# Sharing out the low parts of the expert weights: GpSimd every third half slot, VectorE the others

## The reference

```python
def moe_swiglu(h, router_w, w_gu, w_down):
    probs = jax.nn.softmax((h @ router_w).astype(jnp.float32), axis=-1)
    top_p, top_i = lax.top_k(probs, TOP_K)
    top_p = top_p / jnp.sum(top_p, axis=-1, keepdims=True)
    ...
    for e in range(N_EXPERTS):
        y = y + gates[..., e:e + 1] * swiglu(h, w_gu[e], w_down[e])
```

## Time and profile before

| | |
|---|---|
| median of 3 runs | 2228.12 us (2222.12 to 2228.62) |
| span of the profiled execution | 2218.5 us |
| mean granted TensorE clock | 0.969 of full speed |
| the experts, first to last matmul | 1422.5 to 2159.8 us |
| busy PE / PEld | 2013.3 / 1505.1 us (91% / 68%) |
| busy DVE / ACT / POOL | 957.6 / 734.1 / 775.3 us |
| bytes moved | 320.03 MB |

### The profile page before, as it was taken

The page is one execution under the profiler, slowest core; times in us unless marked ns, Lnnn a source line. Parts: engine busy times, 40 slices in busy tenths (PEclk is TensorE's granted clock), DMA queues, the critical chain, the costliest instruction groups (busy, mean ns, idle before and its releaser), DMA issues. The chain is left out here.

```text
span 2218.5 us, 38581 instructions
## 1 busy us (share of the span) xinstructions
PE 2013.3 (91%) x14384; PEld 1505.1 (68%) x14385; DVE 957.6 (43%) x1610; ACT 734.1 (33%) x1216; POOL 775.3 (35%) x475
## 2 busy tenths in 40 slices
PE   5999999999998699999999998889999899899990
PEld 2446776777676546888788876667786686678770
DVE  2204665666566445432412228553333434332228
ACT  1112332243233102222122211454445545544331
POOL 0016324422442202112112223564446546543234
PEclk7999999999999899999999999999999999999995
DMA  7212234223321434324322350886658758765354
GB/s 259 76 53 88 82 95 128 82 73 108 120 74 61 162 114 132 105 86 136 114 96 86 100 178 5 282 295 183 209 181 268 242 180 276 245 191 167 110 176 151
DMA packets 257672, 320.03 MB, mean 144 GB/s; under 512 B 25401, under 2 KB 197697, under 8 KB 257435
## 3 DMA queue, kind: packets, MB, share of 16 engines
q1 hardware_dynamic: 242571, 285.01, 40.2%
q10 hardware_dynamic: 10832, 16.96, 2.2%
q0 software_dynamic: 4032, 14.68, 1.7%
HBM read 283.93 MB, written 32.65 MB: 143 GB/s over the span
## 5 line engine op out<-in xcount | busy, mean ns | idle before, releaser
L1335 POOL TENSOR_TENSOR wlo<-wring,whi 128x1024 fp32r<-128x1024 f32 x182 | 462.6, 2544 | 748.8 <-ACT whi L1771 685.1
L1121 PE MATMUL pp<-whi,xTh 128*128 128x512 f32 (+1 forms) x1152 | 446.4, 387 | 29.2 <-POOL wlo L1335 10.2
L1771 ACT ACTIVATE whi<-wring 128x1024 fp32r<-128x1024 f32 (+1 forms) x324 | 315.1, 980 | 438.5 <-PE pp L1123 361.3
L1123 PE MATMUL pp<-wlo,xTh 128*128 128x512 f32 (+1 forms) x1152 | 431.3, 374 | 0.0
L1122 PE MATMUL pp<-whi,xTl 128*128 128x512 f32 (+1 forms) x1152 | 430.4, 374 | 0.0
L2356 DVE TENSOR_TENSOR wlo<-wring,whi 128x1024 fp32r<-128x1024 f32 (+1 forms) x180 | 223.9, 1244 | 207.5 <-ACT whi L1771 120.8
L1121 PEld LDWEIGHTS pp<-whi,xTh 128*128 128x128 f32 x1152 | 218.1, 189 | 85.6 <-POOL wlo L1335 21.7
L1123 PEld LDWEIGHTS pp<-wlo,xTh 128*128 128x128 f32 x1152 | 217.9, 189 | 39.4
L1122 PEld LDWEIGHTS pp<-whi,xTl 128*128 128x128 f32 x1152 | 218.7, 190 | 34.0
L1121 PE MATMUL pp<-whi,hTh 128*128 128x512 f32 x528 | 212.2, 402 | 7.7 <-POOL wlo L1335 2.9
L739 PE MATMUL pp<-xT,wring 128*128 128x512 f32 x384 | 205.0, 616 | 2.0 <-ACT scratch L1572 2.0
(11 more groups left out here) (316 smaller groups left out, 2667.0 us busy)
## 6 DMA issues: line engine op xcount, KB each, us to landing
wring<-in_moe_w_gu SPq DMA_DIRECT2D x320, 256.0 KB, 3.9
wring<-in_ada_w SPq DMA_DIRECT2D x80, 512.0 KB, 4.5
wring<-in_moe_w_down SPq DMA_DIRECT2D x160, 256.0 KB, 3.4
wring<-in_ffn_w_gu SPq DMA_DIRECT2D x80, 256.0 KB, 3.1
wring<-in_dn_w_in SPq DMA_DIRECT2D x96, 128.0 KB, 3.3
wring<-in_ffn_w_down SPq DMA_DIRECT2D x40, 256.0 KB, 3.0
expert_in<-zeros SPq DMA_DIRECT2D x36, 256.0 KB, 3.2
wring<-in_ada_w SPq DMA_DIRECT2D x32, 256.0 KB, 5.9
```

The lines of the kernel that those rows point to most:

```text
L1121: pe.matmul(out, hi[:, c0 + c, tt], wh, start=(first and c == 0), stop=False)
L1123: mm = pe.matmul(out, hi[:, c0 + c, tt], wl, start=False, stop=(last and c == nk - 1))
L1335: pool.tensor_tensor(wlo[:, hs, 0:nk, 0:w], wring[:, ring_p.slot(k), 2:2 + nk, 0:w], whi[:, hs, 0:nk, 0:w].bitcast(F32), ALU.subtract).the ...
L1771: act.activation(whi[:, hs, 0:nk, 0:w], wring[:, ring_v.slot(k), 2 * s:2 * s + nk, 0:w], ACT.Copy)\
```

## The change

Each half of an expert's weights has one maker by its number: GpSimd if m % 3 == 2, VectorE otherwise, over all eight experts (36 halves each, and 36 is a multiple of 3). Two semaphores, `low_by_dve` and `low_by_pool`, replace the pair of the layer, and `low_count` says which count half m of expert e has; PE, SP's fills and its end wait by them. The first lows are 0, 1 and 3 on VectorE and 2 on GpSimd. On VectorE the third low of a group comes ahead of `products`. In the down part a VectorE low of half 28 + m stands at step m itself. The `If`s of `silus` are nested: the first tile that the expert doesn't have ends the test. Layer 0's dense part keeps the even/odd split.

```diff
+def pool_half(m):
+    return m % 3 == 2
+
+def low_count(m, e=0):
+    if pool_half(m):
+        return m // 3 + 1 + e * 12
+    return m + 1 - (m + 1) // 3 + e * 24
...
@@ sync, fill @@
-                    if l is not None:
-                        sp.wait_ge(slot_split[l][half], k + 1 + i * per)
+                    if l == 0:
+                        sp.wait_ge(slot_split[half], k + 1 + i * per)
+                    elif l and (i or k >= RING):
+                        sp.wait_ge(low_sem(2 * k + half), low_count(2 * k + half - 2 * RING, i))
...
@@ tensor, half @@
-                    pe.wait_ge(slot_split[l][s], split_count(k, e))
+                    if l:
+                        pe.wait_ge(low_sem(m), low_count(m, e))
+                    else:
+                        pe.wait_ge(slot_split[s], split_count(k, e))
...
@@ gpsimd @@
-            low_halves(1, 0, 2)
+            low(1, 2, 0, low_by_pool)
...
-            low_halves(1, 2, 146)
+            for i in range(5, 292, 3):
+                low(1, i % 36, i // 36, low_by_pool)
...
@@ scalar, silus @@
-                        if t == 0 or l == 0:
+                        if l == 0:
                             one()
-                        else:
-                            with act.If(n > t):
-                                one()
+                    if l:
+                        def deeper(t):
+                            b = t if j % 2 == 0 or t > 1 else 5 + t
+                            act.wait_ge(f["gu_ps"], q0 + (t + 1))
+                            act.activation(hbuf[:, t, 0:w], bank(b)[:, 0:w], ACT.Silu).then_inc(f["sil_done"], 1)
+                            if t + 1 < T:
+                                with act.If(n > t + 1):
+                                    deeper(t + 1)
+                        deeper(0)
...
@@ vector, expert @@
+                def own_lows(lo, hi, e):
+                    for m in range(lo, hi):
+                        if not pool_half(m):
+                            low(m // 2, e, m % 2)
...
-                        low(2 * j + 2, e)
+                        if l:
+                            own_lows(4 * j + 4, 4 * j + 7, e)
+                        else:
+                            low(2 * j + 2, e)
                         products(c * 6 + n * j, n, j)
-                        low(2 * j + 3, e)
+                        if l:
+                            own_lows(4 * j + 7, 4 * j + 8, e)
+                        else:
+                            low(2 * j + 3, e)
...
-                        if m % 2 and (l or e == 0 or m < 8):
+                        if l:
+                            own_lows(28 + m, 29 + m, e)
+                        elif m % 2 and (e == 0 or m < 8):
                             low(14 + m // 2, e)
...
@@ vector, ahead of the router @@
-            for k in range(2):
-                dve.wait_ge(S["slot_hi"], hi_count(1, 2 * k))
+            for m in (0, 1, 3):
+                k, s = m // 2, m % 2
+                dve.wait_ge(S["slot_hi"], hi_count(1, m))
```

More of the change, by code:

```diff
@@ L332, in backbone, with low_sem @@
                                           "xTh_ready", "xTl_ready") if l or n not in ("xs_in", "y_out")} for l in range(2)]
-        slot_split = [[sem(f"slot_split_{half}{l}") for half in ("first", "second")] for l in range(2)]
+        slot_split = [sem(f"slot_split_{half}") for half in ("first", "second")]
+        low_by_dve, low_by_pool = sem("low_by_dve"), sem("low_by_pool")
+        def low_sem(m):
+            return low_by_pool if pool_half(m) else low_by_dve
         yg_in = [sem(f"yg_in{t}") for t in range(T)]
@@ L585, in _ @@
                 for half, pieces in enumerate(parts(ring.slot(k))):
-                    for split in slot_split[0]:
+                    for split in slot_split:
                         sp.wait_ge(split, 37 + k)
@@ L620, in _ @@
             for k in range(2):
-                for split in slot_split[1]:
-                    sp.wait_ge(split, k + 1 + 18 * 8)
-                for half in slot_loaded[ring.slot(k)]:
+                for s, half in enumerate(slot_loaded[ring.slot(k)]):
+                    sp.wait_ge(low_sem(2 * k + s), low_count(2 * k + s - 2 * RING, 8))
                     sp.sem_inc(half, 32)
@@ L1324, in _, with low @@
             pool.wait_ge(S["pool_const"], 1)
[L1326 to L1341, removed]
+            def low(l, m, e, done):
+                k, s = m // 2, m % 2
+                nk = half_rows(k, s)
+                w = 256 if k in (10, 11) else 512
+                hs = m % HALVES
+                pool.wait_ge(S["slot_hi"], hi_count(l, m, e))
+                pool.tensor_tensor(wlo[:, hs, 0:nk, 0:w], wring[:, ring_of[l].slot(k), 2 * s:2 * s + nk, 0:w],
+                                   whi[:, hs, 0:nk, 0:w].bitcast(F32), ALU.subtract).then_inc(done, 1)
+            pool.sem_inc(slot_split[1], RING)
             pool.wait_ge(S["pool_const"], 2)
@@ L1458, in _ @@
                 pool.tensor_tensor(rstd[:, 1, t:t + 1], rstd[:, 0, t:t + 1], mhalf[:, 0:1], ALU.pow).then_inc(S["ln_rstd"], 1)
-            low_halves(0, 0, 36)
+            for i in range(36):
+                low(0, 2 * (i % 18) + 1, i // 18, slot_split[1])
             pool.wait_ge(S["gs_in"], 32)
@@ L1964, in _ @@
                     dve.sem_inc(F[l][n], 1)
-                dve.sem_inc(slot_split[l][0], RING)
+            dve.sem_inc(slot_split[0], RING)
             def add_mod(b, out):
@@ L2350, in ffn, with low @@
                 ring_v = ring_of[l]
-                def low(k, e):
+                def low(k, e, s=0):
+                    nk = half_rows(k, s)
                     w = 256 if k in (10, 11) else 512
[L2354 to L2357, removed]
+                    hs = (2 * k + s) % HALVES
+                    dve.wait_ge(S["slot_hi"], hi_count(l, 2 * k + s, e))
+                    dve.tensor_tensor(wlo[:, hs, 0:nk, 0:w], wring[:, ring_v.slot(k), 2 * s:2 * s + nk, 0:w],
+                                      whi[:, hs, 0:nk, 0:w].bitcast(F32), ALU.subtract)\
+                        .then_inc(low_by_dve if l else slot_split[0], 1)
+                def own_lows(lo, hi, e):
+                    for m in range(lo, hi):
+                        if not pool_half(m):
+                            low(m // 2, e, m % 2)
                 def xs_low(i, t, g, b):
@@ L2537, in _ @@
             w8 = slice(4, 12)
-            for k in range(2):
-                dve.wait_ge(S["slot_hi"], hi_count(1, 2 * k))
-                dve.tensor_tensor(wlo[:, 2 * k, :, :], wring[:, ring_of[1].slot(k), 0:2, :],
-                                  whi[:, 2 * k, :, :].bitcast(F32), ALU.subtract).then_inc(slot_split[1][0], 1)
+            for m in (0, 1, 3):
+                k, s = m // 2, m % 2
+                dve.wait_ge(S["slot_hi"], hi_count(1, m))
+                dve.tensor_tensor(wlo[:, m, :, :], wring[:, ring_of[1].slot(k), 2 * s:2 * s + 2, :],
+                                  whi[:, m, :, :].bitcast(F32), ALU.subtract).then_inc(low_by_dve, 1)
             dve.wait_ge(S["once_ps"], 7 + T)
```

## The result

Over 20 runs of each, the changed kernel takes 2229.0 us (2225.83 to 2235.95) and the kernel before 2225.1: **ratio 1.0021, 95% interval 1.0014 to 1.0029**. So it is 0.2% slower, some 4 us: within the 0.3% that the prediction called no change, though clear of 1. Predicted were 11.2 us less. The profiled execution spans 2226.8 us and took 2228.6, 1.8 more. The 9.6 us that the prediction had added to the span of before was thus no constant: the execution profiled there was a short one (with the same 1.8 it took an estimated 2220.3 us). Single profiles must be read with that in mind: of the 8.3 us between the two spans only about 4 are the change.

The account below looks back on a forecast made before the run. In one-tile experts, GpSimd's and VectorE's lows taking turns, with transfers close behind. Capped by transfers, gate/up saves 5.4, 2.9 and 2.1 us, down 0.5 and 0.3, sum 11.2, other terms 0: 2228.1 to 2216.9 us, range 2203 to 2228.

Parts of the forecast that it names:

- What bounds the kernel: One-tile experts 0, 3 and 5: PE's weight loads wait 26.1 us for GpSimd's lows, which take turns with VectorE's; transfers close behind.
- So the floor of the turns falls from at most 39.8 to about 35.2: One-tile gate/up: four full turns go from 2.24 to 1.08, 4.6 us less; 13.9 over three if nothing else were close.
- At most 2.22 if GpSimd has its turn, still hidden: Experts of two or three tiles: a VectorE low blocked by GpSimd takes at most 2.22 us, hidden behind PE's 2.7 per half.
- Transfers, the cap: One-tile stretches shrink only until the DMA share is 0.95: gate/up 5.4, 2.9, 2.1 us less, down 0.5, 0.3; sum 11.2.
- VectorE's order: Gate/up's third low ahead of products, refill asked for earlier; in experts of two or three tiles nothing gained or lost.
- rival B: One-tile down parts: nine VectorE lows at 1.23 ahead of xTl eat the gain, 11.1, or refills stay late; 2228.0; chance 0.20.
- Nested silus: ACT's tests in the experts: one instead of four with one tile; at most 7.4 us of ACT time, counted as 0.
- SP's queue: Refill transfers keep number and order, cost 0; a late VectorE low delays later refills by at most 2.22 us per ring turn.
- Ahead of the router: VectorE makes three lows instead of two, 5.5 us, 1.0 more, hidden in its 2.15 us of idle time.
- Experts of more tiles: Experts of two or three tiles: lows hidden behind PE, nothing gained or lost; two-tile stretches stay at 65 us.
- rival C: The lows ahead of xTl also bite in experts with more tiles: 27.1 over 22 steps, less 11.2; 2244.0 us; chance 0.08.
- Rival A: No cap: transfers go over 0.95, PE becomes the bound in gate/up; 22.0 us less, 2206.1; chance 0.22.

Follow-up runs that it names:

- half the bytes: Each expert weight transfer loads half its bytes, the rest of the slot keeps what lay there; ratio to before 0.9948 on the kernel before, 0.9972 on the changed kernel.
- the down order: In the down part VectorE makes hTl and xTl ahead of the step's low: changed kernel 1.0009, all lows on VectorE 0.9964, ratios to before.
- the two pairs of the table: Without and with the down order: changed kernel 1.0021 and 1.0009; all lows on VectorE 0.9994 and 0.9964.

## Why the prediction was wrong

The sign of the forecast was wrong, and 2229.0 lies 1.0 us past the upper end of its range. Its outcome "within 0.3%" had 0.22. By its own steps:

**What bounds the kernel** held: the largest moves were in experts 0, 3 and 5, and GpSimd's lows were on the path there. Taking away their reading was worth 10.2 us.

**"So the floor of the turns falls from at most 39.8 to about 35.2": this step failed.** It priced the exchange as throughput, 1.66 against 1.47 us a half. But the turns don't run back to back; in a one-tile gate/up part they stand in a ring with the transfer, ACT's high part and PE's matmuls, each waiting for the last. The gate/up parts fell by 2.5 us where the sum had 10.4 of its 11.2. What counts there is who is blocked when, and the blocking hardly shrank, from 56.1 to 52.2 us; PE's waits for lows stayed at 20 us (the prediction's outer bound, 34.7, was read from the weight loads' waits; PE's own were 20.1). The price of the turns on the whole was 10.2 us before and 11.6 after, where the sum had 11.2 to 13.9 less. Worse, a GpSimd that is blocked holds up only its own low; a blocked VectorE holds up hTl, the products and xTl behind it. "At most 2.22 if GpSimd has its turn, still hidden" was granted for experts of two and three tiles and priced nowhere for those of one tile, and in expert 3 alone VectorE stood blocked for 11.6 us instead of 4.3.

**"Transfers, the cap" was never reached**, and with it went the size of the sum. The gate/up share stayed at 0.88, and with half the bytes the split cost the same 0.24%. As a figure for full, 0.95 was fair: the gate/up parts of the version with all lows on VectorE and the down order, where no turns are left, have 0.93 and 0.96 in experts 0 and 3. In that version the next limit may well be as close as the prediction said; under the changed kernel's turns and order nothing pressed against it.

**"VectorE's order" at 0 failed too:** the down parts of one tile grew by 8.0 us. The forecast left it to rival B, which had the right place and mechanism. Rival B priced nine lows at 1.23, 11.1 us; the runs show 6.7 us where VectorE makes all lows and some 2.7 (not resolved by itself) in the changed kernel. It also missed that step 0 puts a low ahead of the last hTl, and so PE's wait for hTl at L1104 went from 0.3 to 5.0 us. Here is that place in expert 3, VectorE, then PE:

```profile
1727.63 3.23 DVE L2382 TENSOR_TENSOR wlo<-wring,whi 128x1024 fp32r<-128x1024 f32 x2 [0.94 <-ACT whi L1790]
1730.78 0.28 DVE L2402 TENSOR_TENSOR hTl<-pp,hTh 128x128 f32 x1
```

```profile
1731.11 0.66 PE L1104 MATMUL pp<-cm,x 128*128 128x128 f32 x4 [0.76 <-DVE hTl L2402]
```

Two lows stand ahead of hTl, 3.23 us together where two free ones take 2.44, and PE idles for 0.76 us. In the kernel before only one low, half 26's, stands between the last products and hTl.

**Nested silus at 0** held (0.9997). **SP's queue at 0** is contradicted by no run, but the chain after has 7.5% for SP (L461) where before had 2.7%: that points to refills held behind a late low of VectorE, but it wasn't tried by itself. **Ahead of the router** held: the three lows took 5.65 us, 5.5 expected. **Experts of more tiles** held within 2 us (544.3 to 546.2), and rival C did not come. But its steps are not free there: the down order takes 1.6 and 3.7 us off these experts in the two pairs of the table. **Rival A** failed even with the transfers' cap out of play: at half the bytes, the split still gained nothing.

**Of the signs listed**, the number of GpSimd's lows (96) and the 65 us stretches came as said. The mean of these lows over both widths, which the earlier trace rows gives as 2.54, went to 2.16 instead of staying near 2.5: a third of them are narrow now, and the full ones fell from 2.77 to 2.55. The weight loads' wait for GpSimd halved, but to 12.7 us, not under 10. The stretches of 34 to 38 us and the share of 0.95 did not come. Gate/up near 40 us with a share under 0.90 was the stated sign of rival B, and that is what came. That B's 2228.0 is 1.0 us off is in part luck: it took a gain of 11.2 us that never arose, and set the whole of its 11.1 us against it.

What stays open: how the changed kernel's loss divides between blocking and order (PE's waits put 6.3 us ahead of the transpositions, the order by itself gave back 2.7, and the single steps are near what a run resolves), and what holds the one-tile gate/up parts at 35.4 us on average (106.1/3), over PE's 32.6, once turns and transfers are both eased; VectorE's lows still have 10.2% of that chain and ACT's high part 4.6%. Whether the order in the changed kernel matters through SP's refills or through PE's xTl alone wasn't tried either.

## What to carry to other kernels

Before work is moved between two engines that exclude each other, count not only the turns but who will be blocked in them and what is queued behind that engine: a wait on a helper that does nothing else is cheap, the same wait on the engine that feeds PE in four ways is not. If two engines that exclude each other differ twofold in speed and the faster one has room, try giving it all of the work, with the moved work behind the operations that PE waits for; here the two together turned 0.2% slower into 0.4% faster. A row of waits can also change its releaser without any change in the wait: look at its longest entries before you compare two totals. When several shares of a stretch stand at 0.6 to 0.9 and none at 1, suspect a chain in series and test it by easing two of them apart and together: here the savings added up, and the floor worked out from one pair's throughput predicted a gain that didn't come.

## What the runs showed of the hardware

- A fill by GpSimd (MEMSET, 128x1024, 0.954 us) doesn't hold up VectorE's lows: their mean beside fills is 1.224 us, as against 1.221 with no GpSimd lows. A GpSimd low, which reads two operands, holds one up until it is done (3.08 us in the timeline above).
- The two engines' blocking is not shared evenly. With one low each in turn GpSimd bore 41.5 of 56.1 us; with one GpSimd low to two of VectorE's, VectorE bore 42.9 of 52.2.
- A transfer with half the bytes doesn't land in half the time. Median from issue to landing of the gate/up transfers, kernel before and then with half the bytes:

```profile
wring<-in_moe_w_gu SPq DMA_DIRECT2D x320, 256.0 KB, 3.9
```

```profile
wring<-in_moe_w_gu SPq DMA_DIRECT2D x320, 128.0 KB, 2.3
```

128 KB less save 1.6 us of 3.9; by a straight line through the two, an estimate, 0.7 us would be left at no bytes at all. So halving the bytes takes away 1.6 us, not the whole of the transfer's place in the chain.
